# GpSimd picks the expert numbers of a head between its gathers, and the best sums are searched among 136 in place of 256

## The chip, the core and the metric

The kernel runs on one core of a Trainium2 chip. Its engines are named as in the profile: PE (TensorE), DVE (VectorE), ACT (ScalarE), POOL (GpSimd) and SP (SyncE, which here only issues DMAs). The metric is the device time of one execution in microseconds; a comparison takes the median of several.

## The reference

Two decoder layers over 256 tokens of width 1024, in float32. Each layer has a gated mixer (pooling and causal attention) and then PEER, a retrieval over 128 x 128 single-neuron experts. The mixer matters here only as work that shares the engines; the change is in PEER:

```python
q = (xc @ w_q).reshape(TOKEN_CHUNK, PEER_HEADS, 2, PEER_HALF)
s = jnp.einsum('thpd,pkd->thpk', q, sub_keys)          # 8 heads, 2 sides, 128 keys
sv, si = lax.top_k(s, PEER_TOPK)                       # 16 best keys of each side
cand = sv[:, :, 0, :, None] + sv[:, :, 1, None, :]     # 16 x 16 sums
cand_id = si[:, :, 0, :, None] * PEER_NKEYS + si[:, :, 1, None, :]
cv, ci = lax.top_k(cand.reshape(..., 256), PEER_TOPK)  # 16 best sums
eid = jnp.take_along_axis(cand_id.reshape(..., 256), ci, axis=-1)
g = jax.nn.softmax(cv, axis=-1)
act = jax.nn.gelu(jnp.einsum('thkd,td->thk', u[eid], xc))
y = jnp.einsum('thk,thkd->td', g * act, v[eid])
```

So every token reads 8 x 16 = 128 rows of u and of v at numbers that its own scores give. Both lists of `sv` come sorted, the largest first.

## The kernel before, in words

The 256 tokens are two tiles of 128 (a token to a partition), so with two layers there are four *windows* w = 0 to 3. A window has 128 gathers (8 heads of 16 experts): gather g brings, for each of the 128 tokens, one 8 KB row of u and v side by side, 1 MB in all, into one of the seven slots of `ring` (RING = 7). Two gathers make a *tick*, 64 ticks a window.

One gather goes through the engines like this. POOL waits until the slot's last row has been used, then issues the indirect DMA (L1372). DVE takes the dot product of the u half with the token (`dot`, L1208). ACT makes the GELU and the weight in five short steps (`scalar_row`, L892 to L900). Most rows are then summed by PE: ACT spreads the weight on a diagonal (L910), and PE multiplies it with the v half into `ybank` (L691), which frees the slot. On ticks in which PE has other work, one of the two rows is summed by DVE instead (`weighted`, L1221).

Beside this stream, and woven into it by hand, runs everything else: the mixer and the query projections of the *next* window, whose weight chunks SP loads, and the search for that window's experts. Each engine's program is a set of Python generators that yield the tick at which their next piece is due (`vector_mix`, `scalar_mix`, `tensor_mix`; `streamed` and `advance` put the pieces behind the rows of that tick). The ticks of a head's steps are in the lists `first_heads` (window 0), `later_heads` and `last_heads`; `head_tick(w, h, step)` reads them, two ticks between a head's steps.

For one head DVE does, in this order:
- `key_search` (L942, L945, L939): the 16 best keys of each side out of `score`, into `sv` and `si`, eight at a time: maximum, their places, replace them, again.
- `sum_search`: `all_sums` (L953, L955) writes the 256 sums over the head's own scores, which lie in `buf1`, and casts `si` to `sif`; then the same search over 256 columns, and `places` splits each place into row and column (`cab`, L960, L961, cast at L963).
- `mark` (L984): 2 x 16 x 16 one-hot rows in the tile `both`, where `cabf` equals 0 to 15.
- `pick` (L991, L993): multiplies them with `sif` and sums each row of 16, into `picked`.
- `experts` (L998, L1006): first number x 128 + second, plus the layer's offset, cast to the numbers in `expert`, which raises `expert_ready`. For the last head of all it also makes `last_halves` (L1003).
- `weigh_heads` (L1034, L1036): the softmax weights.

The first head of window 0 is done in two halves of eight (`first_experts`), since the stream can't start before it. POOL waits on `expert_ready` before a head's first gather, and ACT waits on it before it overwrites the score tile with the gates of the next mixer (`gate`, L733).

## Time and profile before

| | us |
|---|---|
| median of 3 runs | 1548.58 (1547.98 to 1548.90) |
| the profiled execution | 1548.52 |
| its span, first to last instruction | 1546.7 |
| busy: PE / DVE / ACT / POOL | 1274.5 / 1136.4 / 913.0 / 661.5 |
| of POOL: 508 gathers of 1282 ns | 651.4 |
| of DVE: 512 dot products of 1224 ns | 624.3 |
| of DVE: 128 weighted sums of 1281 ns | 164.0 |
| moved by DMA | 643.5 MB |

The busy times overlap, so none of them is the time. The page also cuts the span in 40 slices and gives the DMA engines' rate in each, which is the first thing to look at in a kernel that reads this much: the stream of gathers is 537 of the 643 MB. A line of the waits reads "engine, line <- engine, line: us in total, times, longest": who stood still for whom.

### The profile page before, as it was taken

Reading aid. Unit: us, or ns where it says so; the run is one execution under the profiler, and the core shown is the slowest. Engines: PE = TensorE matmul, PEld = TensorE weight load, DVE = VectorE, ACT = ScalarE, POOL = GpSimd, SP = SyncE. Lnnn points to the kernel's source line nnn. Section 1 sums busy time; section 2 is a strip of 40 time slices with the busy share of each in tenths; the row PEclk is TensorE's granted clock in tenths of the full one; section 3 lists DMA queues with packets and bytes.
Section 4 is the critical chain, followed back from the end, with each engine's and each line's share of the span. In section 5 each row is a group of like instructions: output and inputs, shape, how many; then the busy total and the mean of one; then the engine's idle time right before and its main releaser. Section 6 shows DMA issues by size and latency. Waiting matters only on the chain.

```text
span 1546.7 us, 18716 instructions
## 1 busy us (share of the span) xinstructions
PE 1274.5 (82%) x5582; PEld 783.1 (51%) x5582; DVE 1136.4 (73%) x2598; ACT 913.0 (59%) x3311; POOL 661.5 (43%) x520
## 2 busy tenths in 40 slices
PE   8999898876998788756688978797878987788886
PEld 8986566542554465533355546564545532232322
DVE  2159998877888769536788886976778777777555
ACT  2226566567667446434676664655676666666776
POOL 0014344455445333323544542334654555554554
PEclk9999999988899899987799999999989999999999
DMA  9989999999999999999999999999999999999998
GB/s 393 400 335 405 408 413 426 426 427 427 424 421 404 426 427 426 426 426 427 426 414 424 402 427 427 421 426 426 423 426 405 426 427 428 426 427 426 427 411 328
DMA packets 90317, 643.51 MB, mean 416 GB/s; under 512 B 10040, under 2 KB 10600, under 8 KB 12904
## 3 DMA queue, kind: packets, MB, share of 16 engines
q0 software_dynamic: 74304, 536.90, 83.1%
q1 hardware_dynamic: 15588, 105.18, 16.3%
q8 instruction: 44, 0.72, 0.2%
q14 instruction: 57, 0.47, 0.1%
q10 hardware_dynamic: 324, 0.23, 0.0%
HBM read 641.23 MB, written 1.05 MB: 415 GB/s over the span
## 4 chain that ended last, share of the span: by engine, by line
DMA 42%; PE 27%; DVE 17%; ACT 6%; issue 5%; POOL 2%; DVEq 0%; POOLq 0%; ACTq 0%
DMA ring<-in_uv,expert 41%; PE ybank L691 15%; PE bank L486 8%; DVE ring L1208 6%; DVE xs L1221 3%; POOL ring L1372 2%; ACT diag L910 2%; ACT wgt L900 1%; DMA wring<-in_chunks 1%; PE bank L632 1%; ACT th L898 1%; PE bank L621 1%; PE bank L464 1%; DVE si L945 1%; DVE buf L939 1%
## 5 line engine op out<-in xcount | busy, mean ns | idle before, releaser
L1372 POOL DMA_INDIRECT ring<-in_uv,expert x508 | 651.4, 1282 | 867.7 <-PE ybank L691 528.0
L691 PE MATMUL ybank<-ring,diag 128*128 128x512 f32 x1528 | 785.1, 646 | 248.2 <-ACT diag L910 247.2
L1208 DVE SCALAR_TENSOR_TENSOR ring<-ring,tok 128x1024 f32<-128x1024 f32 x512 | 624.3, 1224 | 299.4 <-DMA ring<-in_uv,expert 295.1
L691 PEld LDWEIGHTS ybank<-ring,diag 128*128 128x128 f32 x1528 | 278.9, 199 | 627.4 <-ACT diag L910 403.8
L892 ACT ACTIVATE sq<-dots 128x1 f32<-128x1 f32 x512 | 102.5, 200 | 490.1 <-DVE ring L1208 488.7
L900 ACT ACTIVATE wgt<-th,half_p 128x1 f32<-128x1 f32 x512 | 198.1, 387 | 17.1
L486 PEld LDWEIGHTS bank<-hT,wring 128*128 128x128 f32 x1536 | 185.5, 198 | 34.5 <-issue 30.1
L486 PE MATMUL bank<-hT,wring 128*128 128x128 f32 x1536 | 186.6, 281 | 8.1 <-DMA wring<-in_chunks 7.8
L1221 DVE SCALAR_TENSOR_TENSOR xs<-ring,wgt,xs 128x1024 f32<-128x1024 f32 x128 | 164.0, 1281 | 5.3 <-ACT wgt L900 3.7
L910 ACT ACTIVATE diag<-cst,wgt 128x128 f32<-128x128 f32 x384 | 154.2, 402 | 12.4
L898 ACT ACTIVATE th<-arg,dots 128x1 f32<-128x1 f32 x512 | 150.8, 295 | 16.6
L893 ACT ACTIVATE half_p<-dots,prob 128x1 f32<-128x1 f32 x512 | 142.9, 279 | 0.2
L895 ACT ACTIVATE arg<-sq,gelu_bias 128x1 f32<-128x1 f32 x512 | 142.9, 279 | 0.0
L486 PEld LDWEIGHTS bank<-hT,held 128*128 128x128 f32 x736 | 91.2, 198 | 19.0 <-issue 19.0
L486 PE MATMUL bank<-hT,held 128*128 128x128 f32 x736 | 90.9, 280 | 0.0
L632 PE MATMUL bank<-held,buf 128*128 128x256 f32 x256 | 59.0, 386 | 0.0
L632 PEld LDWEIGHTS bank<-held,buf 128*128 128x128 f32 x256 | 49.8, 196 | 13.6 <-issue 7.1
L486 PE MATMUL bank<-hT,ring 128*128 128x128 f32 x448 | 51.2, 276 | 0.0
L486 PEld LDWEIGHTS bank<-hT,ring 128*128 128x128 f32 x448 | 50.5, 192 | 0.7 <-DMA ring<-in_chunks 0.4
L701 ACT ACTIVATE buf<-bank 128x256 f32<-128x256 f32 (+2 forms) x65 | 28.4, 445 | 31.0 <-PE bank L486 28.4
L1208 DVE DVE_READ_ACCUMULATOR ring<-ring,tok 128x1 f32 x512 | 42.2, 82 | 0.0
L945 DVE FIND_INDEX8 si<-sv,buf 128x8 uint32<-128x128 f32 x128 | 34.9, 285 | 0.0
(143 smaller groups left out, 790.3 us busy)
## 6 DMA issues: line engine op xcount, KB each, us to landing
wring<-in_chunks SPq DMA_DIRECT2D x52, 1024.0 KB, 9.4
held<-in_chunks SPq DMA_DIRECT2D x24, 1024.0 KB, 24.8
ring<-in_chunks SPq DMA_DIRECT2D x20, 1024.0 KB, 12.3
ring<-in_uv,expert POOLq DMA_INDIRECT x508, 11.5
xs<-in_x SPq DMA_DIRECT2D x2, 512.0 KB, 4.4
wpool<-in_w_pool SPq DMA_DIRECT2D x2, 512.0 KB, 13.3
trunk_out<-buf SPq DMA_DIRECT2D x4, 256.0 KB, 4.9
ring<-in_pool_scale SPq DMA_DIRECT2D x1, 512.0 KB, 14.8
```

The costliest lines, as they stand in the source:

```text
L486: ins = pe.matmul(b[:, m * CW + lo:m * CW + lo + P], wt[k][:, lo:lo + P], hT[:, k, :], start=(k == 0), stop=(k == KC - 1))
L632: ins = pe.matmul(b[:, 0:CW], mergedT[:, k, :], wt[k][:, :], start=(k == 0), stop=(k == KC - 1))
L691: ins = pe.matmul(ybank[m][:, :], diag[:, nth % DIAGS, :], ring[:, (2 * t + r) % RING, D + m * BANK:D + (m + 1) * BANK], start=(nth == ten ...
L892: act_stepped(act.activation(sq[:, r:r + 1], dots[:, c:c + 1], ACT.Square))
L893: act.activation(half_p[:, c:c + 1], dots[:, c:c + 1], ACT.Copy, scale=prob[:, 2 * n + r:2 * n + r + 1])
L895: act_stepped(act.activation(arg[:, r:r + 1], sq[:, r:r + 1], ACT.Identity, scale=0.044715 * GELU_C, bias=gelu_bias[:, 0:1]))
L898: act_stepped(act.activation(th[:, r:r + 1], arg[:, r:r + 1], ACT.Tanh, scale=dots[:, c:c + 1]))
L900: ins = act.activation(wgt[:, c:c + 1], th[:, r:r + 1], ACT.Identity, scale=half_p[:, c:c + 1], bias=half_p[:, c:c + 1])
L910: act.activation(diag[:, nth % DIAGS, :], ident, ACT.Copy, scale=wgt[:, c:c + 1]).then_inc(diag_done, 1)
L1208: dve.scalar_tensor_tensor(out=ring[:, g % RING, 0:D], in0=ring[:, g % RING, 0:D], scalar=1.0, in1=tok[:, :], op0=ALU.mult, op1=ALU.mult, ...
L1221: dve.scalar_tensor_tensor(out=total, in0=ring[:, (2 * t + r) % RING, D:2 * D], scalar=wgt[:, c:c + 1], in1=total, op0=ALU.mult, op1=ALU.a ...
L1372: pool.indirect_dma_start(ring[:, g % RING, :], None, uv, bass.IndirectOffsetOnAxis(ap=expert[:, at:at + 1], axis=0)).then_inc(row_landed[ ...
```

## The change

GpSimd gets a part of each head but the first of window 0. DVE still marks the one-hot rows and then raises `marked`. GpSimd, between two gathers, multiplies them with `sif` in place, folds each row of 16 in four additions (8, 4, 2, 1), makes the number and copies it into `expert`, each step behind a wait for the one before. The gather before which it does so is in the table `picks`: `ceil(2 * head_tick(w, h, 2)) + RING`, seven gathers after the tick at which DVE had done it.

The sums are cut. Among two sorted lists the 16 best sums have (i+1)(j+1) <= 16, so rows 8 to 15 matter only with column 0: 8 x 16 + 8 = 136 columns (`likely_sums`). A place from 128 on has its own code: a third row of `cab` and a third marking instruction, and the number of the column-0 key is added to those rows' numbers beforehand, as 1/128 of it. The cast of the places to float is gone. Before it writes the sums, DVE waits for the pick of the head before, since `sif`, `both` and `picked` are used again.

```diff
@@ -61,6 +61,11 @@
 
 NEXT_CHUNKS = (C_K, C_K + 1, C_V, C_V + 1)
 
+
+
+FRONT = TOPK // 2
+SUMS = FRONT * TOPK + FRONT
+
 HEAD_PAIRS = [(hd, hd + 2) for hd in range(HEADS) if hd % 4 < 2]
 HEAD_ORDER = [hd for heads in HEAD_PAIRS for hd in heads]
 
@@ -181,8 +186,7 @@
         sif = sb("sif", [P, 2, TOPK])
         cv = sb("cv", [P, TOPK])
         ci = sb("ci", [P, TOPK], U32)
-        cab = sb("cab", [P, 2, TOPK], U32)
-        cabf = sb("cabf", [P, 2, TOPK])
+        cab = sb("cab", [P, 3, TOPK], U32)
         picked = sb("picked", [P, 2, TOPK])
         cmax = sb("cmax", [P, 1])
         gsum = sb("gsum", [P, 1])
@@ -253,6 +257,8 @@
         top_exp = sem("top_exp")
         prob_ready = sem("prob_ready")
         expert_ready = sem("expert_ready")
+        marked = sem("marked")
+        pool_step = sem("pool_step")
         dve_step = sem("dve_step")
         dot_done = sem("dot_done")
         act_step = sem("act_step")
@@ -960,7 +966,33 @@
                 step(dve.tensor_scalar(cab[:, 0, 0:n], ci[:, 0:n], bits, None, ALU.logical_shift_right))
                 step(dve.tensor_scalar(cab[:, 1, 0:n], ci[:, 0:n], 2 ** bits - 1, None, ALU.bitwise_and))
                 settle(dve)
-                step(dve.tensor_copy(cabf[:, :, 0:n], cab[:, :, 0:n]))
+
+            def likely_sums(sums):
+
+                square = sums[:, 0:FRONT * TOPK].rearrange("p (i j) -> p i j", i=FRONT)
+                step(dve.tensor_tensor(square, sv[:, 0, 0:FRONT].unsqueeze(2).to_broadcast([P, FRONT, TOPK]),
+                                       sv[:, 1, :].unsqueeze(1).to_broadcast([P, FRONT, TOPK]), ALU.add))
+                step(dve.tensor_tensor(sums[:, FRONT * TOPK:], sv[:, 0, FRONT:],
+                                       sv[:, 1, 0:1].to_broadcast([P, FRONT]), ALU.add))
+                step(dve.tensor_copy(sif[:, :, :], si[:, :, :]))
+                settle(dve)
+
+                step(dve.scalar_tensor_tensor(out=sif[:, 0, FRONT:], in0=sif[:, 1, 0:1].to_broadcast([P, FRONT]),
+                                              scalar=1.0 / NK, in1=sif[:, 0, FRONT:], op0=ALU.mult, op1=ALU.add))
+
+            def likely_places():
+
+                step(dve.tensor_scalar(cab[:, 0, :], ci[:, :], 4, None, ALU.logical_shift_right))
+                step(dve.tensor_scalar(cab[:, 1, :], ci[:, :], FRONT * TOPK + TOPK - 1, None, ALU.bitwise_and))
+                step(dve.tensor_scalar(cab[:, 2, :], ci[:, :], FRONT * TOPK + FRONT, None, ALU.bitwise_xor))
+                settle(dve)
+
+            def likely_mark(lo, n, hot):
+                for side, code, from_, to in ((0, 0, 0, FRONT), (0, 2, FRONT, TOPK), (1, 1, 0, TOPK)):
+                    step(dve.tensor_tensor(hot[:, side, :, from_:to],
+                                           cab[:, code, lo:lo + n].unsqueeze(2).to_broadcast([P, n, to - from_]),
+                                           iota16[:, from_:to].unsqueeze(1).to_broadcast([P, n, to - from_]),
+                                           ALU.is_equal))
                 settle(dve)
 
             def maximum():
@@ -968,20 +1000,23 @@
 
             def sum_search(h, eight):
 
-                cand = score[:, 2 * h:2 * h + 2, :].rearrange("p a k -> p (a k)")
+                cand = score[:, 2 * h:2 * h + 2, :].rearrange("p a k -> p (a k)")[:, 0:SUMS]
                 if eight == 0:
-                    all_sums(cand.rearrange("p (i j) -> p i j", i=TOPK), TOPK)
+
+                    if PH * w + h:
+                        dve.wait_ge(expert_ready, experts_of(w, h - 1) if h else experts_of(w - 1, PH - 1))
+                    likely_sums(cand)
                     if PH * w + h:
                         dve.wait_ge(top_exp, PH * w + h)
                 search(lambda r: cv[:, :], lambda r: ci[:, :], lambda r: cand, range(1), (eight,))
                 if eight:
                     maximum()
-                    places(TOPK, 4)
+                    likely_places()
 
             def mark(lo, n, hot):
 
                 best = hot.shape[3]
-                step(dve.tensor_tensor(hot, cabf[:, :, lo:lo + n].unsqueeze(3).to_broadcast([P, 2, n, best]),
+                step(dve.tensor_tensor(hot, cab[:, 0:2, lo:lo + n].unsqueeze(3).to_broadcast([P, 2, n, best]),
                                        iota16[:, 0:best].unsqueeze(1).unsqueeze(1).to_broadcast([P, 2, n, best]),
                                        ALU.is_equal))
                 settle(dve)
@@ -998,11 +1033,6 @@
                 step(dve.scalar_tensor_tensor(out=picked[:, 0, these], in0=picked[:, 0, these], scalar=float(NK),
                                               in1=picked[:, 1, these], op0=ALU.mult, op1=ALU.add))
                 settle(dve)
-                if w == windows - 1 and h == PH - 1:
-                    for side in range(2):
-                        step(dve.tensor_scalar(last_halves[:, side, :], picked[:, 0, TOPK - HALVED:TOPK], 2.0,
-                                               float(2 * layer * EXPERTS + side), ALU.mult, ALU.add))
-                    settle(dve)
                 dve.tensor_scalar(expert[:, h * TOPK + lo:h * TOPK + lo + n], picked[:, 0, these],
                                   float(layer * EXPERTS), None, ALU.add).then_inc(expert_ready, 1)
 
@@ -1162,7 +1192,7 @@
                 weigh_heads(0)
                 yield head_tick(w, 0, 2)
                 hot = both[:, 0:2 * P].rearrange("p (a k i) -> p a k i", a=2, i=TOPK)
-                mark(8, 8, hot)
+                likely_mark(8, 8, hot)
                 pick(8, 8, hot)
                 experts(0, 8, 8)
             for h in range(0 if w else 1, PH):
@@ -1177,10 +1207,9 @@
                 sum_search(h, 8)
                 yield head_tick(w, h, 2) - 0.5
                 hot = both[:, :].rearrange("p (a k i) -> p a k i", a=2, i=TOPK)
-                mark(0, TOPK, hot)
+                likely_mark(0, TOPK, hot)
+                dve.sem_inc(marked, 1)
                 yield head_tick(w, h, 2)
-                pick(0, TOPK, hot)
-                experts(h, 0, TOPK)
                 weigh_heads(h)
 
         def hand_over(dve, w):
@@ -1351,9 +1380,55 @@
 
             @block.gpsimd
             def _(pool):
+                pool_steps = [0]
+
+                def stepped(ins):
+                    ins.then_inc(pool_step, 1)
+                    pool_steps[0] += 1
+
+                def pool_settle():
+                    pool.wait_ge(pool_step, pool_steps[0])
+
+                def pick_number(w, h):
+
+                    return PH * w + h
+
+                def pick_head(w, h):
+                    layer = w // NT
+                    hot = both[:, :].rearrange("p (a k i) -> p a k i", a=2, i=TOPK)
+                    pool.wait_ge(marked, pick_number(w, h))
+                    stepped(pool.tensor_tensor(hot, hot, sif[:, :, :].unsqueeze(2).to_broadcast([P, 2, TOPK, TOPK]),
+                                               ALU.mult))
+                    pool_settle()
+                    width = TOPK
+                    while width > 2:
+                        width //= 2
+                        stepped(pool.tensor_tensor(hot[:, :, :, 0:width], hot[:, :, :, 0:width],
+                                                   hot[:, :, :, width:2 * width], ALU.add))
+                        pool_settle()
+                    stepped(pool.tensor_tensor(picked[:, :, :], hot[:, :, :, 0], hot[:, :, :, 1], ALU.add))
+                    pool_settle()
+                    stepped(pool.tensor_scalar(picked[:, 0, :], picked[:, 0, :], float(NK), float(layer * EXPERTS),
+                                               ALU.mult, ALU.add))
+                    pool_settle()
+                    stepped(pool.tensor_tensor(picked[:, 0, :], picked[:, 0, :], picked[:, 1, :], ALU.add))
+                    pool_settle()
+                    if w == windows - 1 and h == PH - 1:
+                        for side in range(2):
+                            stepped(pool.tensor_scalar(last_halves[:, side, :], picked[:, 0, TOPK - HALVED:TOPK], 2.0,
+                                                       float(side), ALU.mult, ALU.add))
+                        pool_settle()
+                    pool.tensor_copy(expert[:, h * TOPK:(h + 1) * TOPK], picked[:, 0, :]).then_inc(expert_ready, 1)
+
+
+                picks = {ceil(2 * head_tick(w, h, 2)) + RING: (w, h)
+                         for w in range(windows) for h in range(0 if w else 1, PH)}
+
                 half_rows = uv.rearrange("n (h d) -> (n h) d", h=2)
                 for g in range(windows * HK):
                     w, at = g // HK, g % HK
+                    if g in picks:
+                        pick_head(*picks[g])
                     if g in (0, 1, 8):
                         pool.wait_ge(expert_ready, (0, 1, 8).index(g) + 1)
                     elif at % TOPK == 0:
```

## Rows read from the trace of the kernel before

**Rows 1.** The page: engines busy; GB/s in 40 slices of the span.

```profile
PE 1274.5 (82%) x5582; PEld 783.1 (51%) x5582; DVE 1136.4 (73%) x2598; ACT 913.0 (59%) x3311; POOL 661.5 (43%) x520
...
GB/s 393 400 335 405 408 413 426 426 427 427 424 421 404 426 427 426 426 426 427 426 414 424 402 427 427 421 426 426 423 426 405 426 427 428 426 427 426 427 411 328
```

**Rows 2.** Windows: stretch, us, busy us by engine, clock, DMA share, GB/s.

```profile
129.00:226.00 97.00, 86.40 (x500) 62.81 (x499) 93.18 (x247) 56.74 (x215) 42.26 (x33) 0.96 1.00 413
...
404.00:516.00 112.00, 95.39 (x389) 55.87 (x387) 97.13 (x250) 74.22 (x271) 56.23 (x44) 0.96 1.00 416
...
773.00:902.00 129.00, 112.20 (x461) 66.91 (x460) 108.83 (x264) 88.83 (x317) 59.85 (x49) 0.95 1.00 415
...
1160.00:1224.00 64.00, 57.50 (x244) 34.54 (x244) 51.41 (x115) 43.49 (x163) 30.83 (x25) 0.97 1.00 414
...
1224.00:1482.00 258.00, 209.51 (x505) 81.44 (x503) 185.40 (x443) 175.48 (x642) 134.36 (x106) 1.00 1.01 427
```

**Rows 3.** Waits, 129 to 226 us: total us, times, longest us.

```profile
POOL ring L1372 <- DVE xs L1221: 27.6, 8, 5.6
POOL ring L1372 <- PE ybank L691: 26.0, 14, 4.2
```

**Rows 4.** Groups of DVE: count, total us, ns of one, idle time before.

```profile
L1208 DVE SCALAR_TENSOR_TENSOR ring<-ring,tok 128x1024 f32<-128x1024 f32 x512 | 624.3, 1224 | 299.4 <-DMA ring<-in_uv,expert 295.1
...
L1221 DVE SCALAR_TENSOR_TENSOR xs<-ring,wgt,xs 128x1024 f32<-128x1024 f32 x128 | 164.0, 1281 | 5.3 <-ACT wgt L900 3.7 <-DVE wpool L1120 0.2
...
L942 DVE MAX8 sv<-buf 128x8 f32<-128x128 f32 x128 | 31.1, 284 | 4.5 <-ACT buf L701 3.3
...
L942 DVE MAX8 cv<-buf 128x8 f32<-128x256 f32 x64 | 27.4, 428 | 2.2
...
L945 DVE FIND_INDEX8 ci<-cv,buf 128x8 uint32<-128x256 f32 x64 | 26.8, 419 | 0.0
...
L984 DVE TENSOR_TENSOR both<-cabf,cst 128x512 f32<-128x512 f32 x31 | 21.4, 689 | 0.0
...
L991 DVE TENSOR_TENSOR both<-both,sif 128x512 f32<-128x512 f32 x31 | 21.3, 686 | 0.0
...
L993 DVE TENSOR_REDUCE picked<-both 128x32 f32<-128x512 f32 x31 | 21.3, 686 | 1.1
...
L939 DVE MATCH_REPLACE8 buf<-cv,buf 128x256 f32<-128x256 f32 x32 | 13.1, 409 | 0.0
...
L1006 DVE TENSOR_SCALAR expert<-picked 128x16 uint32<-128x16 f32 x31 | 5.7, 184 | 1.1
```

**Rows 5.** Issue to landing of gathers: whole run, 129:226, 404:516, 773:902, 1224:1482.

```profile
DMA to landing us min/median/max: 5.4/11.5/29.0
...
DMA to landing us min/median/max: 6.3/10.1/17.3
...
DMA to landing us min/median/max: 7.6/9.6/17.0
...
DMA to landing us min/median/max: 7.5/10.5/14.4
...
DMA to landing us min/median/max: 8.5/11.7/14.1
```

**Rows 6.** Timeline (start, us, instruction): gathers beside a dot and clear of one.

```profile
1496.53 0.94 POOL L1372 DMA_INDIRECT ring<-in_uv,expert  x1 [0.30 <-issue]
...
1510.14 1.22 DVE L1208 SCALAR_TENSOR_TENSOR ring<-ring,tok 128x1024 f32<-128x1024 f32 x1 [1.24 <-DMA ring<-in_uv,expert]
...
1510.54 1.64 POOL L1372 DMA_INDIRECT ring<-in_uv,expert  x1 [0.84 <-PE ybank L691]
```

**Rows 7.** Timeline of POOL: gathers behind a pick, first and last of 14.

```profile
133.63 0.94 POOL L1372 DMA_INDIRECT ring<-in_uv,expert  x1 [2.29 <-PE ybank L691]
...
1205.64 0.94 POOL L1372 DMA_INDIRECT ring<-in_uv,expert  x1 [0.78 <-PE ybank L691]
```

**Rows 8.** Timeline of DVE: the sums of head 3, window 0.

```profile
165.87 0.42 DVE L953 TENSOR_TENSOR buf<-sv 128x256 f32<-128x256 f32 x1
```

## The prediction, before the changed kernel was run

> **What bounds the kernel now.** I read the page's DMA rate first. The reader should see that the DMA engines are never idle for long: between the first rows and the last they move 400 to 428 GB/s, and the slices stop at 427 to 428 [rows 1]. I take 427 GB/s as full. No engine is as full: the largest busy share is PE's 82%, DVE has 73% [rows 1]. So the run is bounded by bytes, and an edit that moves no byte can win only where the rate is under 427.
>
> The windows say where that is. Four stretches are **lean**: 129 to 226 us at 413 GB/s, 404 to 516 at 416, 773 to 902 at 415, 1160 to 1224 at 414 [rows 2]. What they lose is 97 x 14/427 = 3.2 us, 112 x 11/427 = 2.9, 129 x 12/427 = 3.6 and 64 x 13/427 = 1.9: 11.6 us. The others stand at the full rate, as 1224 to 1482 does [rows 2]. In the lean stretches DVE is busy 93.2 of 97 us, 97.1 of 112, 108.8 of 129 and 51.4 of 64, and PE 86.4, 95.4, 112.2 and 57.5 [rows 2]. In the first, GpSimd (POOL), which issues the gathers, waits about as long for DVE's weighted sum as for PE's [rows 3]: a ring slot comes free late because DVE and PE are late. In the other three PE is as full as DVE. The largest single loss, the start up to 129 us, is a chain of weight chunks and first rows that the change hardly touches.
>
> **What DVE loses and gains, for each of 31 heads** [rows 4]. Removed: the multiply (686 ns), the reduction (686), the combination to a number (about 180, as its neighbour) and the cast to expert numbers (184): 1.74 us. The sums shrink from 256 to 136 columns: two maxima go from 428 to about 292 ns (284 at 128 columns), two index searches from 419 to about 293, one replacement from 409 to about 284: 0.65 us. Added: marking goes from one instruction of 512 columns (689) to three of 128, 128 and 256 columns, by the 128 and 256 column maxima about 284 + 284 + 428 = 1.00 us, so 0.31 more; the sums take 284 + two short instructions of about 180 in place of one of about 428, 0.21 more. The third place takes the turn of a cast that is gone: nothing. Three waits of 0.035 us (1.1 us over 31 before the expert cast) go too. Sum: 1.74 + 0.65 + 0.10 - 0.31 - 0.21 = 2.0 us a head, 61 us of DVE's 1136. The first head of all gains 0.5 us before the token row is made; there PE holds the ring slots, so I count 0.5 at most.
>
> **What that is worth.** Nothing at the full rate. In the first lean stretch four heads give DVE 8 of its 93 us; I take 2.5 of the 3.2 us back. In the other three I take 40% of 8.4, 3.4 us, since PE is as late there. With the start: 6.4 us. Bounds are 0 (PE ends last everywhere) and 12.1.
>
> **What POOL gets: the pause.** A pick is eight instructions in a row between two gathers: one multiply of 512 elements, adds of 256, 128, 64 and 32, and three on 16. Each waits for the one before. No row shows such an instruction on POOL, so I bound it. Below: DVE's durations for the same sizes, 0.69 + 0.43 + 0.28 and about 0.2 for each of five, and 0.035 between: 2.7 us. Above: each as long as a gather's own issue (0.94) with the 0.30 that lies between two unhindered ones [rows 6]: 9.9 us. I take 4.5, nearer the lower end, since six of the eight handle at most 128 elements.
>
> Then DVE. A gather that starts while DVE's dot product runs takes 1.64 us, not 0.94: the dot started at 1510.14 and ran 1.22, the gather started at 1510.54 and ended at 1512.18, 0.82 after it [rows 6]. So POOL's work waits out a DVE instruction that reads two operands from SBUF. DVE is in such ones (dots 624.3 us, weighted sums 164.0 [rows 4]) for 788 us, 51% of the span and, as its first 110 us hold none, 55% of the rest. Eight starts that each meet one at 55% and wait out half of 1.22 add 2.7 us; POOL itself holds DVE off during part of that, so I take 1.8. The pause is T = 6.3 us, range 3 to 12.
>
> The Trainium skill (GPSIMD Engine Reference, "Elementwise — side-by-side cycle accounting") puts a two-input operation at about 2.6 cycles an element at 1.2 GHz. By it the 1040 elements would be an estimated 2.3 us, and with eight gaps of 0.30 the pick's own time 4.7; no run here shows it yet.
>
> **Does the pause reach the DMA engines?** What hides it is the backlog. An issued gather lands after 5.4 us at the least and 11.5 in the median [rows 5]; the difference is queue that goes on being served while POOL is away. Besides, the pick sits where POOL would wait for a slot anyhow. So a pause is hidden up to L = (idle before the next gather) + (median landing - 5.4), and T - L shows as a hole. The picks' places follow from the code's tick lists (gather 13, 23, ... 473). Fourteen fall into lean stretches. Their idle times are 2.3, 1.8, 1.4, 0.3; 0.7, 0.3, 2.8, 3.3; 0.3, 0.8, 2.9, 5.6; 0.6, 0.8 (first and last of the 14 in [rows 7]). The landings there, 10.1, 9.6, 10.5 and as I take it 10.2 [rows 5], leave 4.7, 4.2, 5.1 and 4.8. So L is 7.0, 6.5, 6.1, 5.0; 4.9, 4.5, 7.0, 7.5; 5.4, 5.9, 8.0, 10.7; 5.4, 5.6. At T = 6.3 the holes sum to 7.6 us. But DVE, earlier by 2.0 us a head, frees slots sooner and lets the queue grow; with 1 us more of it they sum to 1.5. I take 2.0. The other 17 cost nothing: eleven fall where weight chunks fill the queue too, and the six from 1224 us on have L of at least 6.3 + 0.3 [rows 5]. What this cover is worth: without it each pick would cost its whole pause, 31 x 6.3 = 195 us.
>
> **DVE pays for POOL's reads** as POOL for DVE's, if the lock works both ways: I put 1.0 us on the first stretch's return.
>
> **Waits added.** DVE, before a head's sums, now waits for POOL's pick of the head before; dots and weighted sums are queued behind it. The one tight place is the third pick's forerunner: the pick starts near 158 us, ends near 164, and DVE reaches the next sums at 165.87 [rows 8], a little earlier after the change. I price it at 0.2 and up to 2 us. ScalarE waits before it overwrites the score tile with the second tile's last gates; it will be held some 6 us near 293 us, with three rows behind it, in a stretch with a long queue: nothing, and 3 us without that queue. GpSimd's wait for the mark costs nothing, since the mark lies about two rows ahead of the pick. No DMA is moved but the gathers behind each pick.
>
> **Sum.** -6.4 + 1.0 + 2.0 + 0.2 = -3.2. The profiled execution took 1548.52 us (span 1546.7), and the median of the three is 1548.58, so the sum needs no correction: 1545.3 us.
>
> **Rivals.**
> - *The pause is too long.* T decides, and the point is about 7 us. At 7 the holes (L raised by 1) sum to 5.3 and eat the gain: 1548.6. At T = 8 they sum to 13.7 us, at 9 to 32, now with the six late picks. So 8 us give 1548.5 - 5.2 + 13.7 = 1557 us, and 9 give 1575. For it: every one of eight starts can meet a dot. Against it: six of eight are tiny, and two thirds of the picks lie under a longer queue.
> - *Gain and holes cancel* (T near 7, or PE ends last in the lean stretches): 1548.5, from 1546 to 1551.
> - *The lock takes back what DVE was given.* While POOL reads, DVE's dots wait. If POOL holds it for 2.3 us a pick, that is more than the 2.0 saved. The return of 5.9 us in the lean stretches is gone, only the start's 0.5 stays, and L is not raised, so the holes come nearer to 7.6; I take 4: 1548.5 - 0.5 + 4 = 1552 us. It decides once POOL's reads exceed 2 us a head. The Trainium skill (SBUF — State Buffer, "SBUF: two separate sides") says that whichever starts first holds the shared pair and the other fully blocks. The trace agrees on one side, as the 1.64 us gather shows; no row shows DVE blocked.
>
> **How the numbers follow.** Forecast case 0.38 (its own range 1542 to 1548), cancelling 0.24, too long a pause 0.28, the lock 0.10. A difference of 0.2%, 3.1 us, is about what a measurement of this kernel can tell from none. Faster: 0.33 of the first and 0.03 of the second, 0.36. Within: 0.05 + 0.19 + 0.03 of the lock = 0.27. Slower: 0.02 + 0.28 + 0.07 = 0.37. The range must take in a pause near 8 us and, below, T near 4 with a full return: 1541 to 1563.
>
> **What would show it.** Right: DVE busy near 1075 us; picks of about 6 us from the first multiply to the expert copy; the lean stretches at 418 to 424 GB/s; DVE's waits for POOL under 3 us. Wrong: the rate falls at the picks' places (418, 448, 1177 and 1205 us first), picks over 7 us, dots longer than 1.22 us, or POOL's waits for PE unchanged in the lean stretches, which would put the limit on PE.

## The result and the profile after

The changed kernel takes 1587.98 us in the median (1581.65 to 1591.85), the kernel before beside it 1548.74: a ratio of 1.0249, 95% interval 1.0236 to 1.0262. That is 39 us slower where 1545.3 was forecast, and outside the range of 1541 to 1563. The profiled execution took 1581.65 us, its span is 1579.8, 33 us more than before's. One of pause_40's four executions, below, fell in the chip's slower state (1751 us, at a mean granted clock of 0.69 in place of 0.94), so its median is that of the other three.

The page of the changed kernel, engines and rate:

```profile
span 1579.8 us, 18940 instructions
PE 1282.5 (81%) x5582; PEld 788.0 (50%) x5582; DVE 1103.4 (70%) x2599; ACT 914.4 (58%) x3311; POOL 842.2 (53%) x770
GB/s 396 399 336 361 403 424 415 426 427 427 401 366 401 426 427 426 426 427 427 426 426 376 411 426 426 427 425 426 427 424 375 353 405 413 404 399 410 406 426 339
...
L1237 DVE SCALAR_TENSOR_TENSOR ring<-ring,tok 128x1024 f32<-128x1024 f32 x512 | 650.8, 1276 | 369.2 <-DMA ring<-in_uv,expert 365.0
L1250 DVE SCALAR_TENSOR_TENSOR xs<-ring,wgt,xs 128x1024 f32<-128x1024 f32 x128 | 169.0, 1320 | 5.6 <-ACT wgt L906 3.7
```

The bytes are the same (643.5 MB) and their rate is not: beside [rows 1], slices 4, 11 to 13, 22 and all from the 31st to the 38th stand at 353 to 413. DVE is 33 us less busy, and a dot product is 52 ns longer [rows 4]. The same windows as [rows 2]:

```profile
129.00:226.00 97.00, 83.58 (x475) 59.89 (x473) 83.92 (x228) 51.76 (x194) 61.11 (x63) 0.95 0.95 392
404.00:516.00 112.00, 92.08 (x372) 53.48 (x371) 87.00 (x227) 73.67 (x271) 75.10 (x68) 0.97 0.94 388
773.00:902.00 129.00, 107.03 (x451) 64.28 (x449) 105.48 (x256) 85.21 (x312) 81.39 (x74) 0.96 0.99 406
1160.00:1224.00 64.00, 55.03 (x223) 33.30 (x222) 47.89 (x127) 41.62 (x155) 32.88 (x33) 0.92 0.96 394
1224.00:1482.00 258.00, 204.09 (x512) 84.08 (x510) 171.43 (x426) 163.77 (x603) 167.12 (x157) 0.97 0.97 397
```

The four lean stretches got leaner, 388 to 406 in place of 413 to 416, and the last one, forecast to cost nothing, fell from 427 to 397. PE and DVE are less busy in the four, so neither is what holds the rows up. What is new on POOL, grouped by form (busy us, mean ns | idle before):

```profile
L1406 POOL TENSOR_TENSOR both<-both 128x256 f32<-128x256 f32 x31 | 43.3, 1397 | 2.4
L1400 POOL TENSOR_TENSOR both<-both,sif 128x512 f32<-128x512 f32 x31 | 41.4, 1337 | 0.8
L1406 POOL TENSOR_TENSOR both<-both 128x128 f32<-128x128 f32 x31 | 32.1, 1036 | 2.4
...
L1414 POOL TENSOR_TENSOR picked<-picked 128x16 f32<-128x16 f32 x31 | 16.8, 543 | 2.6
...
L1411 POOL TENSOR_SCALAR picked<-picked 128x16 f32<-128x16 f32 x31 | 10.9, 352 | 2.7
```

All eight forms (667, 589 and 383 ns are the others' means) sum to 195.3 us, 6.3 a pick, and with the seven gaps inside one 6.87. From the end of one gather to the start of the next a pick's place now takes 7.13 us in the mean, against 2.77 before. The forecast had 6.3. A 256-element addition is dearer than the 512-element multiply, which shows that the mean is no cost of the work alone. Here is a pick that met one dot, its three additions by form, and then a pick that met several dots:

```profile
205.51 1.27 POOL L1400 TENSOR_TENSOR both<-both,sif 128x512 f32<-128x512 f32 x1
206.86 2.48 POOL L1406 TENSOR_TENSOR both<-both 128x256 f32<-128x256 f32 x3
207.74 1.44 DVE L1237 SCALAR_TENSOR_TENSOR ring<-ring,tok 128x1024 f32<-128x1024 f32 x1 [3.06 <-DMA ring<-in_uv,expert]
...
210.31 0.20 POOL L1421 CAST expert<-picked 128x16 uint32<-128x16 f32 x1
...
L1406 POOL TENSOR_TENSOR both<-both 128x64 f32<-128x64 f32 x1 | 1.2, 1155 | 0.1
L1406 POOL TENSOR_TENSOR both<-both 128x256 f32<-128x256 f32 x1 | 0.7, 720 | 0.1
L1406 POOL TENSOR_TENSOR both<-both 128x128 f32<-128x128 f32 x1 | 0.4, 449 | 0.1
...
129.47 1.28 POOL L1400 TENSOR_TENSOR both<-both,sif 128x512 f32<-128x512 f32 x1
130.83 4.22 POOL L1406 TENSOR_TENSOR both<-both 128x256 f32<-128x256 f32 x3
```

The first goes from 205.51 to 210.51: 5.0 us, with its addition of 64 elements held under the dot of 207.74, for 1.16 us where the same addition takes 0.29 in other picks. The other ended at 138.97: 9.5 us. The eight instructions at their shortest (1.27, 0.72, 0.45, 0.29, 0.24, 0.20, 0.22 and 0.20 us) and the gaps between them make 4.1 us. None of the 31 picks was that short: each was held at least once, and 2.7 of the mean 6.87 us are waits. Now the pick at gather 445, in the last stretch, on all engines:

```profile
1388.15 1.56 POOL L1447 DMA_INDIRECT ring<-in_uv,expert  x1 [0.86 <-PE ybank L697]
1389.74 1.27 POOL L1400 TENSOR_TENSOR both<-both,sif 128x512 f32<-128x512 f32 x1
1390.12 1.98 DVE L1237 SCALAR_TENSOR_TENSOR ring<-ring,tok 128x1024 f32<-128x1024 f32 x1 [0.86 <-DMA ring<-in_uv,expert]
1391.09 3.36 POOL L1406 TENSOR_TENSOR both<-both 128x256 f32<-128x256 f32 x3
1394.98 1.23 DVE L1237 SCALAR_TENSOR_TENSOR ring<-ring,tok 128x1024 f32<-128x1024 f32 x1 [1.21 <-DMA ring<-in_uv,expert]
1395.13 1.15 POOL L1414 TENSOR_TENSOR picked<-picked 128x16 f32<-128x16 f32 x1
...
1396.70 1.00 POOL L1447 DMA_INDIRECT ring<-in_uv,expert  x1 [0.15 <-issue]
```

Both sides of the lock are here. The dot at 1390.12 begins under POOL's multiply and takes 1.98 us in place of 1.22; POOL's addition of 16 numbers begins under the dot of 1394.98 and takes 1.15 us in place of 0.22. The Trainium skill (SBUF — State Buffer, "SBUF: two separate sides") says that whichever of the two starts first keeps the shared pair for its whole instruction; the trace agrees, in both directions. The rate around this pick, in windows of 3 us:

```profile
1392.00:1395.00 3.00, 1.79 (x5) 0.57 (x4) 1.36 (x5) 2.69 (x11) 2.68 (x5) 1.00 1.03 434
1395.00:1398.00 3.00, 2.65 (x7) 0.83 (x5) 1.79 (x3) 2.18 (x8) 2.40 (x4) 1.00 0.95 401
1398.00:1401.00 3.00, 2.48 (x5) 0.97 (x6) 1.80 (x3) 1.66 (x7) 2.41 (x2) 1.00 0.86 284
1401.00:1404.00 3.00, 2.55 (x7) 0.96 (x6) 1.42 (x9) 1.66 (x6) 2.37 (x3) 1.00 0.88 270
```

Up to 1395, five us into the pause, DMA runs at 434 GB/s on what is queued; it falls to 401 and 284 while the last gather's bytes come in, and it is still at 270 when those of the first new gather do. The landings of the last gather before the pick and the two after it, and of the first gather after the picks at 13, 125 and 370 (the gather's own line, then its landing):

```profile
L1447 POOL DMA_INDIRECT ring<-in_uv,expert x1: 1562/1562/1562, 1388.2 to 1388.2; - x1
DMA to landing us min/median/max: 11.7/11.7/11.7
L1447 POOL DMA_INDIRECT ring<-in_uv,expert x1: 997/997/997, 1396.7 to 1396.7; - x1
DMA to landing us min/median/max: 6.9/6.9/6.9
L1447 POOL DMA_INDIRECT ring<-in_uv,expert x1: 1469/1469/1469, 1398.0 to 1398.0; - x1
DMA to landing us min/median/max: 9.0/9.0/9.0
...
DMA to landing us min/median/max: 8.0/8.0/8.0
...
DMA to landing us min/median/max: 6.7/6.7/6.7
...
DMA to landing us min/median/max: 5.5/5.5/5.5
```

The three about gather 445 land at 1399.9, 1403.6 and 1407.0, 3.7 and 3.4 us apart; the next, 9.6 us after its start at 1399.78, comes 2.4 later. At the full rate a megabyte takes 2.46, so 2.2 us are lost, over two gathers. Of the twenty exposed places (fourteen lean, six late), sixteen show a hole of over 1 us by the measure below. There the first gather landed in 5.5 to 8.9 us, 6.1 in the middle, five of them in 5.5 or 5.6, and the gather behind each in 6.8 to 10.0, 8.0 in the middle. The prediction had taken 5.4. Counted as at gather 445, the first gathers came 26 us late in sum and the ones behind them another 11 (gather 23 is left out, where 1 MB of weights lay between).

**A measure of holes.** For each of the 31 places I take the rate in the 18 us that begin 2 us after the last gather before it, and count 18 x (1 - rate/427). Before: 7.7 us in sum. After: 47.5, which is 39.8 more; the rest of the run lost 7 less, and the span grew by 33. Of the 39.8 the fourteen places in the lean stretches have 27, the six late ones 11.4, and the eleven under weight chunks 1.3. The count overstates the span's growth by 4 to 7 us in the changed kernel and in each of the pause runs from 5.05 us on, so it shows where the time goes rather than how much.

### The profile page after: what moved, and what is told of

Read it like the earlier page. It is cut to its first block, busy times and chain, and to the rows that moved or that the text cites. A ratio compares the mean times of both kernels' runs of the same rounds, so it can differ in the third digit from the quotient of the medians.

```text
span 1579.8 us, 18940 instructions
## 1 busy us (share of the span) xinstructions
PE 1282.5 (81%) x5582; PEld 788.0 (50%) x5582; DVE 1103.4 (70%) x2599; ACT 914.4 (58%) x3311; POOL 842.2 (53%) x770
## 4 chain that ended last, share of the span: by engine, by line
DMA 43%; PE 23%; DVE 14%; POOL 10%; ACT 6%; issue 5%; DVEq 0%; POOLq 0%; ACTq 0%
DMA ring<-in_uv,expert 42%; PE ybank L697 12%; PE bank L492 7%; DVE ring L1237 6%; POOL ring L1447 4%; POOL both L1406 3%; DVE xs L1250 2%; ACT diag L916 1%; DMA wring<-in_chunks 1%; PE bank L638 1%; POOL both L1400 1%; ACT wgt L906 1%; ACT th L904 1%; PE bank L627 1%; DVE si L951 1%
## 5 line engine op out<-in xcount | busy, mean ns | idle before, releaser
L1447 POOL DMA_INDIRECT ring<-in_uv,expert x508 | 636.5, 1253 | 702.1 <-PE ybank L697 396.4
L1237 DVE SCALAR_TENSOR_TENSOR ring<-ring,tok 128x1024 f32<-128x1024 f32 x512 | 650.8, 1276 | 369.2 <-DMA ring<-in_uv,expert 365.0
L1250 DVE SCALAR_TENSOR_TENSOR xs<-ring,wgt,xs 128x1024 f32<-128x1024 f32 x128 | 169.0, 1320 | 5.6 <-ACT wgt L906 3.7
L1406 POOL TENSOR_TENSOR both<-both 128x256 f32<-128x256 f32 (+2 forms) x93 | 96.1, 1033 | 7.3
```

Source lines behind the costliest of these rows:

```text
L1237: dve.scalar_tensor_tensor(out=ring[:, g % RING, 0:D], in0=ring[:, g % RING, 0:D], scalar=1.0, in1=tok[:, :], op0=ALU.mult, op1=ALU.mult, ...
L1250: dve.scalar_tensor_tensor(out=total, in0=ring[:, (2 * t + r) % RING, D:2 * D], scalar=wgt[:, c:c + 1], in1=total, op0=ALU.mult, op1=ALU.a ...
L1406: stepped(pool.tensor_tensor(hot[:, :, :, 0:width], hot[:, :, :, 0:width], hot[:, :, :, width:2 * width], ALU.add))
L1447: pool.indirect_dma_start(ring[:, g % RING, :], None, uv, bass.IndirectOffsetOnAxis(ap=expert[:, at:at + 1], axis=0)).then_inc(row_landed[ ...
```

## The experiments

The theories, once the result was known. **Pause**: POOL's absence between two gathers outlasts the queue, at the fourteen lean and the six late places. **Lock**: GpSimd's reads hold up DVE's dots (and dots the gathers), whatever the pause. **New wait**: DVE or ACT waits for a pick. **Sums**: something in the 136-column search. All runs stand beside the kernel before on the same chip; "before + x" is the difference of the medians.

### One half of the change at a time

*sums_only*: 136 sums and three marks, but DVE picks as before; POOL only gathers.

```diff
-                    if g in picks:
-                        pick_head(*picks[g])
...
+                pick(0, TOPK, hot)
+                experts(h, 0, TOPK)
```

> The 136 sums and the three markings stay, but DVE multiplies, sums and makes the numbers again, and GpSimd only gathers. Holes theory (the time comes from GpSimd's pause of about 6.9 us a pick, during which no gather is issued): all of the loss goes, and what is left is DVE lighter by about 0.25 us a head, so 1545 to 1549 us. Theory that the shorter sums or the extra marking do harm: 1553 us or more. DVE busy near 1129 us, dots at 1224 ns as before.

Measured: 1548.79 us against 1549.03, ratio 1.0002 (0.9993 to 1.0011).

*pick_only*: GpSimd picks, the sums stay at 256 columns (the reverse edit).

> The other half alone: GpSimd picks as in the changed kernel, DVE searches all 256 sums and marks in one instruction. Holes theory: the loss of the changed kernel, 1582 to 1592 us, since the pauses are the same. If the new sums had a share in the loss, it is lower by that share.

Measured: 1588.51, ratio 1.0256 (1.0241 to 1.0272), before + 39.5; gaps of 7.14 us at the picks' places. The whole loss is the pick's, and the sums are worth nothing that could be told from zero.

### A pause without reads

*pause_write*: the kernel before, with 36 tiny memsets at the 31 places, each waiting for the one before. They read nothing, and DVE keeps all its work.

```diff
+                    if g in picks:
+                        for i in range(36):
+                            stepped(pool.memset(idle[:, :], 0.0))
```

> The kernel before, with GpSimd kept busy at the places of the 31 picks by 36 memsets of five columns, each waiting for the one before (about 6 to 7 us by 0.10 us each and a gap of 0.08); they read no SBUF, and DVE keeps all its work. Holes theory: as slow as the changed kernel or slower, 1580 to 1600 us at a pause near 6.5 us, with dots at 1224 ns. Lock theory (DVE's dots wait out GpSimd's reads, and that is where the time goes): under 1555 us, since nothing here reads.

Measured: 1565.41, ratio 1.0117 (1.0099 to 1.0136), before + 16.4, with a pause of 6.34 us. That is between what either theory expected, and less than the pick costs, but the pick is longer. So the same with 40 and with 28 memsets:

*pause_40*:

> The 31 pauses without a read, as long as the picks are in the changed kernel: 40 memsets, 7.0 us. If the length of the pause is all, this is as slow as the changed kernel, 1580 to 1590 us, a steep step from the 1565 at 6.3 us. If the rest of the loss comes from DVE's dots held by GpSimd's reads in the same moments, it is 1570 to 1575 us: 31 times 0.7 us at most more than at 36 memsets, where they show.

Measured: 1584.34, before + 35.9, ratio 1.0238 (1.022 to 1.0257), with pauses of 6.98 us. Its page:

```profile
GB/s 392 392 336 372 401 415 417 423 427 427 393 369 399 426 426 426 426 427 427 426 422 359 426 426 426 426 426 427 427 426 384 361 400 414 404 401 411 404 426 334
L1372 POOL MEMSET warm<- 128x5 f32 x1240 | 128.0, 103 | 69.2
```

Laid beside the changed kernel's slices, it is the same picture: 369 in the 12th, 359 in the 22nd, 384 and 361 in the 31st and 32nd, 400 to 414 after them. Here no dot is longer (1225 ns). Of the 39 us, 36 are to be had by absence alone. The lock isn't needed for the rest either: these pauses are 0.15 us shorter than the picks' mean gap of 7.13, and by the step from pause_38 to pause_40 below (8 us for 0.32) that is an estimated 4 us. What is left to it as a cause of its own lies within the scatter.

*pause_28*:

> The same with 28 memsets, 4.9 us, which is what a pick takes when no dot is in its way (5.0 us). Holes theory with a cover of about 5 us: 1550 to 1555 us. With the prediction's cover: no difference from before, within 2 us.

Measured: 1556.58, ratio 1.0049 (1.0033 to 1.0064), before + 8.1, with pauses of 5.05 us, the length of the shortest picks. Those still met a dot: what the expectation calls a pick with no dot in its way would be 4.1 us. This prices the lock's indirect part: dots stretch a pick from 4.1 to 6.9 us, and of that the step from 5.05 to 6.98 us alone costs 28.

*pause_38*, run later, lies between 36 and 40:

> The kernel before with 38 memsets of 5 columns at the 31 places, a pause of about 6.66 us in the gap, between the 36 that cost 17 us and the 40 that cost 37 us. If holes open place by place with the cover there, as the model with a landing of 7.0 us on an emptied queue says, the cost lies in the middle: 1571 to 1579 us. If there is a step (a pause that reaches past some fixed moment makes the next gather miss more than its own lateness), the cost is near one of the two: under 1568 or over 1582 us.

Measured: 1576.31, ratio 1.0178 (1.0159 to 1.0196), before + 27.8, with 6.66 us. No step, but a steep slope: + 8, 16, 28 and 36 us at 5.05, 6.34, 6.66 and 6.98.

### Where the cover ends

*dose*: pauses at the six late places alone, one length each.

```diff
+                DOSES = {403: 12, 417: 20, 431: 28, 445: 36, 459: 44, 473: 52}
```

> The kernel before, with GpSimd pauses of growing length (12, 20, 28, 36, 44 and 52 memsets of five columns, about 2.1, 3.5, 4.9, 6.3, 7.8 and 9.2 us) at the last window's six pick places, gathers 403, 417, 431, 445, 459 and 473, and nowhere else. The prediction's cover (a queue of 11.7 - 5.4 us) says that the rate stays at 427 GB/s up to the fourth and falls first at the fifth. If the cover is shorter, as the 1.3 to 2.5 us holes at 7 us in the changed kernel say, the third already shows a hole, and from there one grows by 1 us for each us of pause.

One execution: 1555.53 us, span 1553.7. The windows of 18 us behind the pauses of 3.77, 5.08, 7.61 and 8.93 us:

```profile
1295.90:1313.90 18.00, 13.95 (x30) 4.90 (x29) 11.98 (x31) 12.96 (x48) 10.62 (x16) 1.00 1.01 424
1330.20:1348.20 18.00, 12.71 (x26) 4.36 (x26) 11.29 (x30) 11.84 (x45) 9.98 (x24) 1.00 0.99 388
1400.30:1418.30 18.00, 11.87 (x25) 4.06 (x24) 10.27 (x29) 9.95 (x36) 10.03 (x39) 1.00 0.96 367
1437.90:1455.90 18.00, 12.71 (x27) 4.33 (x25) 8.14 (x14) 10.52 (x40) 13.29 (x47) 1.00 0.85 344
```

424, 388, 367 and 344 GB/s are holes of 0.1, 1.6, 2.5 and 3.5 us; 2.50 us left 0.1 and 6.34 us 1.2. The cover in this stretch ends near 5 us, where the prediction had at least 6.6. From 5.08 to 8.93 us the hole grows by 1.9 us, half of the 1 us for each us of pause that was expected. A single hole scatters by more than a us: gather 431 with the same pause has 1.6 here and none in pause_28, which left 0 to 1.8 at these six.

*loaded_58*: pauses of 9.9 us, but only at the eleven places where weight chunks are in the queue.

```diff
+                LOADED = ([(0, h) for h in (5, 6, 7)] + [(w, h) for w in (1, 2) for h in (4, 5, 6, 7)])
...
+                        for i in range(58):
```

> The kernel before with a pause of about 10.2 us (58 memsets), longer than any pick, but only at the eleven places of the stretches where weight chunks are queued too and a gather takes 14 to 16 us to land. Corrected cover (landing there less the 7.0 us of an emptied queue, plus POOL's own idle time of about 5 us: 12 us): no hole, 1548 to 1551 us. If a pause costs what it has over some 5 us wherever it stands, 11 times 5: about 1600 us.

Measured: 1551.39, ratio 1.0025 (1.0016 to 1.0034), before + 3.1, with holes at three of the eleven (2.4, 2.2 and 1.9 us). Of 109 us of pause 3 are paid. What the prediction said of these eleven stands: under the picks they showed holes of 1.3 us in sum.

### What DVE's relief is worth

*relief*: sums_only without DVE's multiply, reduction and combination, and POOL only gathers: the gain without the pause. The numbers are the first head's plus a constant.

```diff
-                pick(0, TOPK, hot)
-                experts(h, 0, TOPK)
...
+                dve.tensor_scalar(expert[:, h * TOPK:(h + 1) * TOPK], expert[:, 0:TOPK],
+                                  float(500 * (PH * w + h) if h else 0), None, ALU.add).then_inc(expert_ready, 1)
```

> What DVE's lighter load is worth by itself. The 136 sums stay, and nobody multiplies, reduces or combines: the expert numbers of every head but the first are left out and replaced by the first head's plus a constant, so the same number of rows and bytes is gathered but the output is not the reference's. GpSimd only gathers. The prediction's term was -6.4 us: 1542 us. As the 136 sums alone gave nothing, the other view is that DVE's time is worth nothing while PE and the queue bound the lean stretches: 1547 to 1549 us.

Measured: 1547.25 against 1548.44, ratio 0.9993 (0.9984 to 1.0002). DVE is 63.7 us less busy, and that is worth 1.2 us, or nothing. The lean stretches in it:

```profile
129.00:226.00 97.00, 86.53 (x503) 63.11 (x502) 86.38 (x255) 57.97 (x220) 42.34 (x33) 0.96 1.01 426
404.00:516.00 112.00, 96.04 (x385) 55.81 (x385) 90.59 (x255) 74.84 (x273) 52.22 (x44) 0.95 1.01 420
773.00:902.00 129.00, 110.79 (x459) 66.43 (x458) 100.69 (x270) 90.34 (x322) 63.24 (x50) 0.96 1.01 418
1160.00:1224.00 64.00, 57.19 (x245) 34.81 (x245) 48.10 (x120) 43.07 (x159) 30.77 (x26) 0.97 1.01 413
```

The first came up from 413 to 426, as forecast; the other three by 4, 3 and -1 GB/s. By [rows 2] that makes 3.0 + 1.0 + 0.9 - 0.1 = 4.8 us, but the span is only 1.5 shorter: the rest was lost in other stretches of that execution, partly in the first 96 us, where the edit does little. What two executions differ by is as large as the gain.

*relief_shift* and *sums_shift*: in both, 18 more rows of the second, third and fourth lean stretch are summed by DVE in place of PE.

```diff
+        shared |= {t for lo, hi in ((52, 71), (111, 135), (179, 191)) for t in range(lo, hi, 2)}
```

> DVE relieved as in the run named relief (expert numbers left out and replaced, output not the reference's), and in the lean stretches of windows 1 to 3 eighteen more rows are summed by DVE in place of PE (18 times 1.28 us on DVE, 18 times 1.72 off PE). If PE is what ends last in the lean stretches, they fill up and the time falls by 3 to 6 us below relief's 1547.3. If it is the length of a row's way through the seven slots whoever does it, no change, 1546 to 1549.

> The same eighteen rows moved to DVE in the kernel with the 136 sums and DVE's own picks, whose output is whole. DVE has no time to spare there (97 of 112 us). If PE ends last: 1545 to 1548 us. If DVE then does: 1550 us or more.

Measured: 1547.51, ratio 0.9992 (0.9984 to 1.0001), and 1548.64, ratio 1.0004 (0.9995 to 1.0012). With DVE relieved and PE relieved too, no time came back. The lean stretches did fill a little (relief_shift's last two stand at 423 and 418 GB/s where relief has 418 and 413), but other stretches of the same execution were 1 to 3 GB/s lower. So it isn't the case that PE alone stood where DVE had stood; why a fuller lean stretch brings no time is not shown by any run.

### The pick spread, or cut

*spread4*: the changed kernel, the pick in four parts before four gathers in a row.

```diff
-                    if g in picks:
-                        pick_head(*picks[g])
+                    for part in picks.get(g, ()):
+                        part()
```

> The changed kernel, with a pick cut in four parts (multiply; add 8; add 4 and 2; the rest) that stand before four gathers in a row from one gather earlier on; two parts for heads 2, 3 and 7 of the first window. Same instructions, same reads, same work off DVE. Holes theory: a part of 1 to 1.7 us fits in GpSimd's idle time or the queue, so 1544 to 1551 us. Lock theory: the reads are as many, dots stay at about 1276 ns, and the time stays above 1575 us.

Measured: 1553.15, ratio 1.003 (1.0018 to 1.0042). Its dots are as long as the changed kernel's (1279 ns), its picks have the same instructions, and 35 of 39 us are gone. What is left, 4 us, could be the lock or gathers that follow one another too slowly. Hence writes alone, ten memsets before each of four gathers:

*spread_write*:

> The kernel before with four short pauses (10 memsets each, about 1.8 us, no reads) before four gathers in a row, in the places of the spread pick's four parts. It asks what of the 4 us that the spread pick lost is left when nothing holds DVE's dots. Lock theory for that rest: 1548 to 1550 us. If instead even 1.8 us before each of four gathers is too much, 1552 to 1555 us, with the same holes after the first heads of windows 1 to 3.

Measured: 1560.17, ratio 1.007 (1.0057 to 1.0083). Above both ranges expected and worse than spread4, without a read: four gathers spaced by 3.1 us and more fall behind the 2.46 in which one is served. The lock isn't needed to explain what spread4 left. In five thinner parts:

*spread5*:

> The changed kernel with the pick in five parts before five gathers in a row: the multiply, the addition of 8, those of 4 and 2, the last addition with the number, and the rest. It does all of the reference. In four parts it took 4.6 us more than before, with gathers that follow one another by some 3.1 us against the 2.45 us in which the DMA engines serve one. Theory (each part is hidden if the gathers still come as fast as they are served): parts of at most 1.4 us and mostly 0.5 to 0.9 bring the spacing down to about 2.7 us, so the loss falls to 0 to 3 us: 1548 to 1552 us. Rival (GpSimd's reads hold DVE, whose dots are 55 ns longer each in four parts too): no change against four parts, 1552 to 1554 us.

Measured: 1550.65, ratio 1.0019 (1.001 to 1.0028), with gaps of 0.9 to 1.9 us at most places and dots of 1287 ns. That is 2.2 us over before: within what was expected of the spacing, and no faster than before.

*short_pick*: the changed kernel without the four additions, its large multiply kept.

```diff
-                    while width > 2:
...
+                    stepped(pool.tensor_scalar(picked[:, 0, :], sif[:, 0, :], float(NK - 1), float(layer * EXPERTS),
+                                               ALU.mult, ALU.add))
```

> The changed kernel with its marks, its 136 sums and GpSimd's first multiply of 512 elements (which reads two operands and so holds DVE's dots off, and is held off by them) at all 31 places, but without the four additions that fold the rows: the expert numbers are 127 x (row number of the side's j-th key) + (its column number), so they are other experts than the reference's and the output is not the reference's. Left of the pick are four instructions of eight. Worked out from the trace of the changed kernel: 1.34 + 0.24 + 0.22 + 0.20 us and four gaps of 0.08 make 2.3 us alone, some 3.3 us where dots are met. Theory (the loss is the length of the pause, against a queue that empties about 5 us after the last gather was issued): the gaps before the next gather fall to about 4 us, which the six pauses of 3.77 us late in the run show to be covered, and the time is 1547 to 1552 us. Rival (the loss comes from GpSimd's big read holding DVE's dots, or from anything else in the changed kernel beside the length): at least a third of the 39 us stays, over 1560 us, with gaps of 4 us.

Measured: 1551.79, ratio 1.002 (1.001 to 1.0031), before + 3.3, with a mean gap of 4.17 us and dots of 1253 ns. At gather 445 (two more instructions of 0.2 us follow, and the gap is 3.16):

```profile
1365.32 1.27 POOL L1400 TENSOR_TENSOR both<-both,sif 128x512 f32<-128x512 f32 x1
1365.70 1.98 DVE L1237 SCALAR_TENSOR_TENSOR ring<-ring,tok 128x1024 f32<-128x1024 f32 x1 [0.86 <-DMA ring<-in_uv,expert]
1366.68 1.07 POOL L1403 TENSOR_SCALAR picked<-sif 128x16 f32<-128x16 f32 x1
```

That is 3 us, not a third of 39: with GpSimd's largest read still at all 31 places, a pause that stays short costs almost nothing. None of these versions beats the kernel before by more than the noise.

## Why the prediction was wrong, step by step

- **What bounds the kernel: right.** Bytes do, and a loss shows as a hole in the rate. The losses of the runs with pauses were found there.
- **DVE's work, 61 us less: right, net 33.** The forms came at their prices (136-column maximum 299 ns against 292 forecast, search 293, replacement 283; marks 286, 286 and 419). relief, without the pick, shows 63.7. In the changed kernel dots and weighted sums took 26.5 + 5.0 us of it back.
- **What that is worth, -6.4: the term was too large.** relief measured -1.2 (+0.3 to -2.5). The first stretch returned what I gave it, the other three 1.8 in place of 3.4 us, and the whole less than their sum. The bound of 0 was nearer than the value taken.
- **The pause, T = 6.3: a little short, by its waits.** T is 6.9. The pick's own time is 4.1 us where I took 4.5, and the waits for DVE add 2.7 where I took 1.8. The count of eight starts at 55% had given just that 2.7; the discount for the time in which POOL holds DVE off isn't borne out. With the prediction's own covers, 6.9 in place of 6.3 adds 3 us of holes, so this is not the main error. The Trainium skill (GPSIMD Engine Reference, "Elementwise — side-by-side cycle accounting") gave an estimated 4.7 for the pick's own time; the instructions at their shortest, with their gaps, measure 4.1.
- **The cover L: the step that failed.** It is idle + median landing - 5.4. It counts a pause as hidden as long as the next gather, landing in the shortest time of the whole run [rows 5], is not late, and it has no term for the gather behind that one. The 5.4 belongs to the second gather of all, issued while only the first (5.6) was under way; the third, issued 1.25 us behind it, took 8.1. The landings of before between 96 and 112 us:

```profile
DMA to landing us min/median/max: 5.4/8.1/9.4
```

  The gather behind dose's longest pause (8.93 us) came in 5.6. In the changed kernel the first gather of the sixteen places with a hole needs 6.1 in the middle, not 5.4, and the one behind it is late too: of the 37 us by which landings are late at fifteen of them, that second gather has 11. (Some expectations above say 7.0; the six late places have 5.8 to 7.2.) One number that does for both is 6.7. With it each L falls by 1.3, and at T = 6.9 the fourteen L's make holes of 28 us and the six late ones (L 5.3 to 5.8) 8: 36 us, where 5.4 gives 13. The holes measured are 39.8 us. Taken place by place, with the gap that each pick really left, 6.1 gives 29 us and 6.7 gives 40, with misses of up to 2.3 us at single places. The 6.7 is fitted to this kernel, where the first gathers alone give 6.1, so that the sums agree this well is in part luck. For the other runs:

| pause, us | sum with 6.7 | holes more than before | time more than before |
|---|---|---|---|
| 5.05 | 8 | 15 | 8 |
| 6.34 | 25 | 24 | 16 |
| 6.66 | 31 | 34 | 28 |
| 6.98 | 37 | 40 | 36 |

- **L raised by 1 through DVE's relief: nothing shows it.** The pauses with all of DVE's work in place (pause_40) cost what the real pick costs, less 3 us. This 1 us was worth 6 of the 7.6 us of holes in the sum.
- **The six late picks: wrong, by the same error.** Their L stood 0.3 to 0.8 above T, so a small error in the floor tipped all six: 11.4 us of holes where none was forecast.
- **The eleven under weight chunks: right,** also at 9.9 us but for three. But the prediction's "two thirds of the picks lie under a longer queue" counted the six late ones in, and even so it is 17 of 31.
- **DVE pays for POOL's reads: right in kind,** with + 52 ns a dot, but off the path: pause_40 has no long dot and is as slow to 3 us.
- **Waits added: right.** No wait of DVE for a pick stands among the changed kernel's waits, and ScalarE's for one, forecast at some 6 us near 293 us, is 2.7.
- **The rivals.** "The pause is too long" came true, at 6.9 in place of its 8 us, and at 1588 in place of 1557. Its decision point, 7 us, was the forecast's error over again: with the fitted 6.7 and no raise the fourteen L's give holes of 1.5 us at T = 4.0 and 4.0 at 4.5, against a gain of 1.2, so it lies near 4 us.

**Open.** From 6.34 to 6.98 us the time rises by 19.5 us and the holes by 16. If only the twenty exposed places paid for the added 0.64 us, it would be 13. Why the slope is steeper, and why 6.34 us costs less time than the sum says, no run here settles. Whether the lock adds anything of its own to the last 3 us (39 against 36) isn't shown: the 0.15 us between the two pauses may be all of it, and pause_40 and the pick differ by less than their scatter. A pick without a two-operand read on DVE's side beside it wasn't tried.

## What to carry to other kernels

A pause on the engine that issues the transfers is hidden only by what is queued, less what the next transfers need to land on a thin queue. Count the second transfer behind the pause as well as the first, don't take the smallest landing of the run for either, and count a cover that exceeds the pause by less than the spread of such landings (5.5 to 8.9 us here) as none. An operation beside a shared port costs its own time plus what it meets, and where the cover is short that second part decides (4.1 us became 6.9, and from 5.05 us on that was worth 28 us of the 39). Hand such an engine its work in pieces shorter than the spacing of the transfers (spread5: the same instructions, 2 us in place of 39), and don't pay for relieving an engine that the bytes already hide.

## What the runs showed of the hardware

- GpSimd's operations of 16 or 32 elements on 128 partitions take 0.20 to 0.24 us where no dot holds them, and 0.06 to 0.09 us lie between one and the next that waits for it. A memset of 5 takes 0.10 us and lengthens no dot (1225 ns in pause_40).
- The lock holds one-operand reads on GpSimd too: in short_pick's rows above, the dot of 1365.70 is held by the multiply, runs on to 1367.68, and the TENSOR_SCALAR of 16 elements behind the multiply ends only at 1367.75, after 1.07 us in place of 0.20. It has 901 ns in the mean there, against the changed kernel's 352:

```profile
L1403 POOL TENSOR_SCALAR picked<-sif 128x16 f32<-128x16 f32 x31 | 27.9, 901 | 2.7
```

- A queue of gathers isn't full or empty: the rate falls (401, then 284 GB/s) while the last gather's bytes are still under way, it stays low (270) while the first new gather comes in, that gather lands in 5.5 to 8.9 us, and the one issued 1.3 us behind it can land late too (3.4 us after it at gather 446, at 2.46 us a gather).
